# The last 64 down rows of a 2752-column FFN in a two-block transformer kernel: one 128-row pass over low and high parts in place of 64-row products

## The chip, the cores and the metric

The kernel runs on one core of one Trainium2 chip. The metric is the device time of one execution in microseconds (us). TensorE does the products, VectorE (DVE in the rows) and ScalarE (ACT) everything elementwise, and the Sync queue (SP) issues nearly all loads.

## The reference, cut to what matters

Two transformer blocks run one after the other on `x` of 1 x 256 x 1024 in float32. The first block has two layers, each of an FFN, a mixer and another FFN, so four FFNs of width `D_FF = 2752`:

```
def swiglu(x, w_gate, w_up, w_down):
    return (jax.nn.silu(x @ w_gate) * (x @ w_up)) @ w_down
x = x + 0.5 * swiglu(rms_norm(x, g[0]), ffn_w_gate[layer, 0], ffn_w_up[layer, 0], ffn_w_down[layer, 0])
```

`w_gate` and `w_up` are 1024 x 2752, `w_down` is 2752 x 1024. The second block has two more FFNs, of width 2816. 2752 is 21 times 128 and 64 more; 2816 is 22 times 128.

## The kernel before, in words

Each weight is read once, in units of at most 128 x 1024 floats (512 KB). `plan` lists the units in the order of their use. For each unit u, SP loads it into one of six staging buffers, as soon as unit u-6 has been split (`unit`, L2673 to 2688). ScalarE copies it into a high part `whi` in the rounded format fp32r (`split`, L1239; one of four buffers, so it waits for `used` of unit u-4). VectorE writes the rest into a low part `wlo` (L1733). Activations are held as high and low parts too. `three` (L600 to 602) then makes a product of three matmuls: high by high, high by low and low by high; low by low is left out.

An FFN runs in this order. `norm_T` transposes `xs` (L612) for k = 0 to 7, two transposes of 128 columns each. Ahead of k = 0 TensorE waits for the residual of token tile 1 and output half 0, ahead of k = 4 for that of tile 1 and half 1, which is the last of the four. ScalarE makes the high part `hTh` of each k (L1252), VectorE the low part `hTl` (through the helper at L1742), and the products of the next stage wait for these. Gate and up products follow by pairs of 128 columns. For each pair the hidden values are multiplied, and their high part `fh` (ScalarE, L1306 or L1310) and low part `fl` (VectorE, L1832 or L1840) are stored, transposed, in row tiles f = 0 to 21.

`down` walks the 22 row tiles of `w_down`. Four PSUM banks hold the output (two tiles t of 128 tokens by two halves n of 512 columns). For every row tile there are four groups of three matmuls, in the order n, then t. In the last row tile each group ends its bank, and VectorE adds the bank to `xs` (`residual`, L1742 for the four FFNs in question, L1783 for the mixers and for the first FFN of the second block): four additions, one after the other in VectorE's queue, followed there by the eight `hTl` of the next `norm_T`.

With F = 2752, `row_starts` gives the last unit the rows F-128 to F-1, of which the first 64 repeat rows already used. All operands of the last row tile are therefore cut to partitions 64 to 127 (`low`), in which the up products have also left the last 64 hidden values. The last pair of the up stage is special too (`if f.odd`): it has 128 + 64 columns, and its second half is worked on in partitions 64 to 127 alone.

Of the kernel before, what the change touches and what calls it, by code (L numbers as in the profile page):

```python
# [203 lines left out]
def build(nc, A, out):  # L204
    ctx = ExitStack()
    with ctx:
# [25 lines left out]
        def bk(*user):  # L232
            return PS[:, B.of[user], :]
# [49 lines left out]
        plan = []  # L283
# [34 lines left out]
                plan.append(([(0, cols(wg, k0, k0 + 4, c + 128, F), (4, 128), 0),  # L318
                              (0, cols(wu, k0, k0 + 4, c + 128, F), (4, 128), 64)], 512))

        def row_starts(F):
            r = [i * 128 for i in range(F // 128)]
            if F % 128:
                r.append(F - 128)
            return r

        def plan_down(w, F):
            plan_rows(w, row_starts(F))

        ffns = [(A["ffn_w_gate"][l, s], A["ffn_w_up"][l, s], A["ffn_w_down"][l, s], F1)  # L330
                for l in range(2) for s in range(2)]
# [54 lines left out]
        class Ffn:  # L386
            def __init__(self, g, i, gl, coef, c):
                self.g, self.gl, self.coef = g, gl, coef
                self.nf = len(row_starts(ffns[i][3]))
                self.odd = ffns[i][3] % 256 != 0  # L390
                self.pairs = self.nf // 2
                self.fh = sb(f"fh{i}", [128, 22, S], F32R, c)
                self.fl = sb(f"fl{i}", [128, 22, S], F32R, c)
                self.sg = [sb(f"sg{i}_{j}", [128, 2, 2 * S], c=c) for j in range(2)]

                self.rows = [(self.fh[:, f, :], self.fl[:, f, :],
                              low if self.odd and f == self.nf - 1 else everyrow, ("fl", g, f // 2))
                             for f in range(self.nf)]

        class Attend:  # L400

# [12 lines left out]
        class Even:  # L414
            def __init__(self, c):
                def al(shape, n=itertools.count()):
                    return sb(f"ev_{next(n)}", shape, c=c)

                self.g, self.gl = 1, 1
                self.mh = sb("ev_mh", [128, 8, S], F32R, c)  # L420
                self.ml = sb("ev_ml", [128, 8, S], F32R, c)
                self.u = sb("ev_u", [128, 4, PAD + S], c=c)
                self.acc = sb("ev_acc", [128, 4, S], c=c)
                self.taps = sb("ev_taps", [128, 4, PE_TAPS, 128], c=c)
                self.sq = sb("ev_sqc", [128, 4, S], c=c)
                self.rs = sb("ev_rs", [128, S], c=c)
                self.th = [sb(f"ev_th{i}", [128, 2 * S], c=c) for i in range(2)]
                self.qkv = sb("ev_qkv", [128, 2, 768], c=c)

                self.qT = sb("ev_qT", [128, 4, S], c=c)  # L430
                self.kT = sb("ev_kT", [128, 1, S], c=c)
                self.o = sb("ev_o", [128, 2, 512], c=c)
                self.cwr = sb("ev_cwr", [34, 512], c=c)
                self.hq = sb("ev_hq", [128, 2, 640], c=c)
                self.hr = sb("ev_hr", [128, 2, 8], c=c)
                self.hk = sb("ev_hk", [128, 2, 2], c=c)
                self.cw = sb("ev_cw", [128, 4, 34], c=c)
                self.vr = sb("ev_vr", [128, 4], c=c)
                self.qg = sb("ev_qg", [128, 2], c=c)
                self.sk = sb("ev_sk", [128, 8], c=c)  # L440
                self.skp = sb("ev_skp", [128, 8], c=c)
                qkv, qT, kT, hr = self.qkv, self.qT, self.kT, self.hr
                self.at = Attend("swa", 8, al, lambda h: qT[64 * (h % 2):64 * (h % 2) + 64, h // 2, :],
                                 lambda h: kT[64 * (h % 2):64 * (h % 2) + 64, 0, :],
                                 lambda kt, h: qkv[:, kt, 640 + (h % 2) * 64:704 + (h % 2) * 64],
                                 both_tiles("swa"), lambda t, h: hr[:, t, h:h + 1], self.o, sink=self.skp, apart=True, crossed=True)
                self.rows = [(self.mh[:, 4 + k, :], self.ml[:, 4 + k, :], everyrow, ("swa oT", k // 2))
                             for k in range(4)]
                self.rows += [(self.mh[:, k, :], self.ml[:, k, :], everyrow, ("ev ml",)) for k in range(4)]

        class Odd:
            def __init__(self, c):
                def al(shape, n=itertools.count()):
                    return sb(f"od_{next(n)}", shape, c=c)

                self.g, self.gl = 4, 4
                self.mh = sb("od_mh", [128, 8, S], F32R, c)
                self.ml = sb("od_ml", [128, 8, S], F32R, c)
                self.u = sb("od_u", [128, 4, 16 + S], c=c)
                self.w1 = [sb(f"od_w{i}", [128, 3, 16 + S], c=c) for i in range(2)]  # L460
                self.pl = sb("od_pl", [128, 4, S], c=c)
                self.pw = sb("od_pw", [128, 4, 128], c=c)
                self.qkv = sb("od_qkv", [128, 2, 1536], c=c)
                self.qT = sb("od_qT", [128, 4, S], c=c)
                self.kT = sb("od_kT", [128, 4, S], c=c)
                self.o = sb("od_o", [128, 2, 512], c=c)
                self.hq = sb("od_hq", [128, 2, 1024], c=c)
                self.hr = [sb(f"od_hr{i}", [128, 2, 8], c=c) for i in range(2)]
                self.psc = sb("od_psc", [128, 4], c=c)
                self.qg = sb("od_qg", [128, 2], c=c)  # L470
                qkv, qT, kT, hr = self.qkv, self.qT, self.kT, self.hr[0]
                self.at = Attend("dil", 8, al, lambda h: qT[64 * (h % 2):64 * (h % 2) + 64, h // 2, :],
                                 lambda h: kT[64 * (h % 2):64 * (h % 2) + 64, h // 2, :],
                                 lambda kt, h: qkv[:, kt, 1024 + h * 64:1088 + h * 64], both_tiles("dil"),
                                 lambda t, h: hr[:, t, h:h + 1], self.o, mult=both_tiles("mult"), apart=True,
                                 late=True)
                self.rows = [(self.mh[:, 4 + k, :], self.ml[:, 4 + k, :], everyrow, ("od ml",)) for k in range(4)]
                self.rows += [(self.mh[:, k, :], self.ml[:, k, :], everyrow, ("dil oT", k // 2)) for k in range(4)]

        class Mixer2:  # L480
            def __init__(self, l, g, c):
# [55 lines left out]

                self.place = [2, 6, 4, 0]
                self.rows = [(self.bh[:, self.place[k // 2] + k % 2, :], self.bl[:, self.place[k // 2] + k % 2, :],
                              everyrow, (P, "low", k // 2)) for k in range(8)]  # L540

            def N(self, a, b, t=None):
                return self.nat[:, :, W0 + a:W0 + b] if t is None else self.nat[:, t, W0 + a:W0 + b]
# [21 lines left out]
        def tensor_program(e):  # L565
# [131 lines left out]
            def down(g, rows, ahead=0):  # L697

                ps = {}
                for t in range(2):  # L700
                    for n in range(2):
                        ps[t, n] = room(("dn", g, t, n))
                for k, (h, lo, sl, step) in enumerate(rows[0:len(rows) - ahead]):
                    u, wh, wl = unit()
                    e.wait_ge(*K.at(*step))
                    last = k + 1 == len(rows)
                    for n in range(2):
                        cols_n = slice(n * 512, n * 512 + 512)
                        for t in range(2):
                            ts = slice(t * 128, t * 128 + 128)  # L710
                            m = three(ps[t, n], h[sl, ts], lo[sl, ts], wh[sl, cols_n], wl[sl, cols_n], k == 0, last)
                            steps = [("dn", g, t, n)] if last else []
                            if t and n:
                                steps.append(("used", u))
                            if steps:
                                m.then_inc(*K.inc("prod", *steps))
                            if last:
                                done("dn", g, t, n)
                        yield

            def ffn(f):
# [39 lines left out]
                for t in range(2):  # L761
                    ts = slice(t * 128, t * 128 + 128)
                    for n in range(2):
                        cols_n = slice(n * 512, n * 512 + 512)
                        for k in range(f.nf - 4, f.nf):
                            h, lo, sl, step = f.rows[k]
                            if k not in us:
                                us[k] = unit()
                                e.wait_ge(*K.at(*step))
                            u, wh, wl = us[k]  # L770
                            w = three(bk("dn", g, t, n), h[sl, ts], lo[sl, ts], wh[sl, cols_n], wl[sl, cols_n], False,
                                      k == f.nf - 1)
                        w.then_inc(*K.inc("prod", ("dn", g, t, n)))
                        done("dn", g, t, n)
# [947 lines left out]
        def vector_program(e):  # L1722
# [77 lines left out]
            def ffn(f):  # L1800
# [23 lines left out]
                def hidden(p):  # L1824
                    s = f.sg[p % 2]
                    e.wait_ge(*K.at("silu", g, p))
                    if f.odd and p == f.pairs - 1:
                        for j, sl in ((0, everyrow), (1, low)):
                            e.tensor_tensor(s[sl, j, 0:256], s[sl, j, 0:256], s[sl, j, 256:512], ALU.mult).then_inc(
                                *K.inc("mult", ("mult", g, p, j)))  # L1830
                            e.wait_ge(*K.at("fh", g, p, j))
                            e.tensor_tensor(f.fl[sl, 2 * p + j, :], s[sl, j, 0:256],  # L1832
                                            f.fh[sl, 2 * p + j, :].bitcast(F32),
                                            ALU.subtract).then_inc(*K.inc("fl", *([("fl", g, p)] if j else [])))
                        return
                    e.wait_ge(*K.at("scaled", g, p, "up"))
# [788 lines left out]
        def sync_program(e):  # L2625
# [51 lines left out]
            def unit(u):  # L2677
# [3 lines left out]
                for i, (off, src, shape, *at) in enumerate(parts):  # L2681
# [2 lines left out]
                        dst = dst.rearrange("p (a b) -> p a b", a=shape[0])  # L2684
                    for c in at:
                        dst = dst[:, :, c:c + src.shape[2]]
                    e.dma_start(dst, src).then_inc(
                        *K.dma(f"st{u % NS}", *([("st", u)] if i + 1 == len(parts) else [])))

# [58 lines left out]
```

## Time and profile before

| what | value |
|---|---|
| three executions, median (lowest to highest) | 1795.98 us (1795.02 to 1800.14) |
| profiled execution, its span; it has no other time | 1791.2 us |
| median less span | 4.8 us |
| TensorE busy | 1775.6 us, 99% |
| VectorE busy | 1272.9 us, 71% |
| ScalarE busy | 948.0 us, 53% |
| DMA queue of the loads | 56.5% of 16 engines |
| granted TensorE clock, mean | 1.000 |

A busy share covers each engine alone. The weight loads of TensorE (PEld) overlap its matmuls (PE), and each matmul's record is longer than the distance to the next one's start, as they are pipelined; so the distance of two starts is the cost of one in a stream.

### The profile page before, as it was taken

What the parts mean: (1) busy time and instruction counts of PE and PEld (TensorE: products, weight loads), DVE (VectorE), ACT (ScalarE), POOL (GpSimd) and SP (SyncE); (2) the same over time, 40 slices, a digit from 0 to 9 for tenths busy, and PEclk for the clock granted to TensorE, in tenths of its full rate; (3) what the DMA queues carried; (4) which work ended last, traced back from release to release, by engine and by line L of the source; (5) the groups of instructions that cost most, each with busy time, mean ns of one, the idle gap of its engine ahead of it and who ended that gap; (6) DMA issues with size and microseconds to landing.
All of it is one profiled execution on the core that took longest, in us unless ns stands there. A gap on an engine that the chain in (4) does not pass through costs nothing.

```text
span 1791.2 us, 24936 instructions
## 1 busy us (share of the span) xinstructions
PE 1775.6 (99%) x9718; PEld 1510.8 (84%) x9718; DVE 1272.9 (71%) x1933; ACT 948.0 (53%) x1346; POOL 30.2 (2%) x39
## 2 busy tenths in 40 slices
PE   9999999999999999999999999999999999999998
PEld 8888878888888888888888788888888878888887
DVE  7774795876577657677656977777756778677774
ACT  6554655555455545555545545455544644555553
POOL 0000000000000001000000000000000000000000
PEclk9999999999999999999999999999999999999999
DMA  8666523666566655366655544556666454456663
GB/s 274 190 181 201 173 71 116 190 177 202 174 195 186 196 166 187 108 200 186 194 177 179 180 119 131 180 181 189 189 192 172 141 156 129 152 188 190 189 195 109
DMA packets 227614, 309.25 MB, mean 173 GB/s; under 512 B 22494, under 2 KB 176254, under 8 KB 227498
## 3 DMA queue, kind: packets, MB, share of 16 engines
q1 hardware_dynamic: 227334, 307.35, 56.5%
q8 instruction: 78, 1.28, 0.3%
q10 hardware_dynamic: 164, 0.30, 0.1%
q14 instruction: 38, 0.31, 0.1%
HBM read 306.57 MB, written 1.05 MB: 172 GB/s over the span
## 4 chain that ended last, share of the span: by engine, by line
PE 91%; DVE 6%; ACT 2%; issue 1%; POOL 0%; POOLq 0%; ACTq 0%
PE ps L649 26%; PE ps L600 15%; PE ps L602 15%; PE ps L601 15%; PE ps L651 13%; DVE wlo L1733 2%; PE ps L1141 1%; PE ps L612 1%; PE ps L816 1%; DVE ev_acc L1742 1%; PE ps L842 1%; ACT whi L1239 1%; PE ps L829 1%; PE ps L784 0%; DVE m_scr L1742 0%
## 5 line engine op out<-in xcount | busy, mean ns | idle before, releaser
L1733 DVE TENSOR_TENSOR wlo<-staging,whi 128x1024 fp32r<-128x1024 f32 (+1 forms) x580 | 692.6, 1211 | 335.7 <-ACT whi L1239 335.3
L1239 ACT ACTIVATE whi<-staging 128x1024 fp32r<-128x1024 f32 (+1 forms) x580 | 606.3, 1050 | 475.5 <-PE ps L602 292.6
L649 PE MATMUL ps<-hT,whi 128*128 128x512 f32 x1984 | 624.1, 396 | 0.1
L651 PEld LDWEIGHTS ps<-hT,wlo 128*128 128x128 f32 x1984 | 372.7, 188 | 88.1
L651 PE MATMUL ps<-hT,wlo 128*128 128x256 f32 x1984 | 389.8, 278 | 0.0
L649 PEld LDWEIGHTS ps<-hT,whi 128*128 128x128 f32 x1984 | 302.1, 189 | 0.5 <-DVE wlo L1733 0.3
L600 PE MATMUL ps<-whi,fh 128*128 128x512 f32 (+1 forms) x520 | 202.8, 390 | 0.0
L601 PE MATMUL ps<-wlo,fh 128*128 128x512 f32 (+1 forms) x520 | 202.3, 389 | 0.0
L602 PE MATMUL ps<-whi,fl 128*128 128x512 f32 (+1 forms) x520 | 202.2, 389 | 0.0
L600 PE MATMUL ps<-whi,hT 128*128 128x512 f32 (+3 forms) x464 | 184.8, 398 | 0.8 <-DVE wlo L1733 0.6
L602 PE MATMUL ps<-whi,hT 128*128 128x512 f32 (+3 forms) x464 | 177.4, 382 | 0.0
L601 PE MATMUL ps<-wlo,hT 128*128 128x512 f32 (+3 forms) x464 | 177.0, 381 | 0.0
L600 PEld LDWEIGHTS ps<-whi,fh 128*128 128x128 f32 (+1 forms) x520 | 97.6, 188 | 21.4 <-DVE wlo L1733 1.4
L602 PEld LDWEIGHTS ps<-whi,fl 128*128 128x128 f32 (+1 forms) x520 | 97.5, 188 | 20.5
L601 PEld LDWEIGHTS ps<-wlo,fh 128*128 128x128 f32 (+1 forms) x520 | 97.6, 188 | 19.9
L600 PEld LDWEIGHTS ps<-whi,hT 128*128 128x128 f32 x464 | 87.2, 188 | 21.4 <-issue 3.8
L602 PEld LDWEIGHTS ps<-whi,hT 128*128 128x128 f32 x464 | 87.2, 188 | 16.3
L1310 ACT ACTIVATE fh<-sg 128x512 fp32r<-128x512 f32 x62 | 39.2, 632 | 114.0 <-DVE sg L1837 114.0
L601 PEld LDWEIGHTS ps<-wlo,hT 128*128 128x128 f32 x464 | 87.4, 188 | 14.3 <-issue 0.5
L1822 DVE TENSOR_TENSOR sg<-sg,R 128x512 f32<-128x512 f32 x124 | 85.9, 692 | 4.3
L1819 DVE TENSOR_TENSOR sg<-ps,sg 128x512 f32<-128x512 f32 x124 | 84.8, 684 | 0.2
L600 PE MATMUL ps<-hT,whi 128*128 128x256 f32 x288 | 82.8, 287 | 0.0
(344 smaller groups left out, 1887.7 us busy)
## 6 DMA issues: line engine op xcount, KB each, us to landing
staging<-in_w_in SPq DMA_DIRECT2D x92, 512.0 KB, 3.7
staging<-in_ffn_w_down SPq DMA_DIRECT2D x88, 512.0 KB, 4.2
staging<-in_ffn_w_gate SPq DMA_DIRECT2D x84, 512.0 KB, 4.5
staging<-in_ffn_w_up SPq DMA_DIRECT2D x84, 512.0 KB, 4.6
staging<-in_w_ffn_gate SPq DMA_DIRECT2D x44, 512.0 KB, 4.5
staging<-in_w_ffn_up SPq DMA_DIRECT2D x44, 512.0 KB, 4.5
staging<-in_w_ffn_down SPq DMA_DIRECT2D x44, 512.0 KB, 4.2
staging<-in_od_w_in SPq DMA_DIRECT2D x16, 512.0 KB, 3.7
```

Of the source, the lines that this page charges most:

```text
L600: e.matmul(o, lh, rh, start=start, stop=False)
L601: e.matmul(o, lh, rl, start=False, stop=False)
L602: return e.matmul(o, ll, rh, start=False, stop=stop)
L612: w = e.transpose(ps[:, t * 128:t * 128 + 128], xs[:, t, k * 128:k * 128 + 128], ident)
L649: e.matmul(o, wh[:, kk, j * 128:j * 128 + 128], hT[:, k, :], start=k == 0, stop=False)
L651: m = e.matmul(o[:, 0:256], wl[:, kk, j * 128:j * 128 + 128], hTh[:, k, :], start=False, stop=k == KD - 1)
L816: w = e.matmul(ops[t][:, (h0 + j) * 64:(h0 + j) * 64 + 64], a.pt[i % 2][:, o:o + 128], a.vN(kt, h0 + j), start=kt == 0, stop=kt == t)
L1239: e.activation(high(u)[:, 0:n], stage[u % NS][:, 0:n], ACT.Copy).then_inc(*K.inc("hi", ("hi", u)))
L1310: e.activation(f.fh[:, 2 * p:2 * p + 2, :], s[:, :, 0:256], ACT.Copy).then_inc(*K.inc("fh", ("fh", g, p, 0)))
L1733: e.tensor_tensor(low_of(u)[:, 0:n], stage[u % NS][:, 0:n], high(u)[:, 0:n].bitcast(F32), ALU.subtract).then_inc(*K.inc("lo", ("lo", u)))
L1819: e.tensor_tensor(ss, PS[:, b:b + 2, 0:256], ss, ALU.add).then_inc(*K.inc("ps_r", *[("ev", u) for u in users]))
L1822: e.tensor_tensor(ss, ss, R22, ALU.mult).then_inc(*K.inc("ps_r", ("scaled", g, p, part)))
```

## The change

The last unit of a 2752-column FFN holds the last 64 rows of `w_down` twice, in partitions 0 to 63 and in 64 to 127, by two DMAs of 256 KB. VectorE writes the low part of the last 64 hidden values not into `fl` but into partitions 0 to 63 of the last tile of `fh`, whose partitions 64 to 127 hold the high part. One product of this tile with `whi` then gives high by high and low by high, and one with `wlo` gives high by low and low by low: two matmuls of 128 rows for each of the four groups, in place of three of 64 rows. The `slice` member of each row entry is dropped. The number of units and their sizes stay.

```
+            plan_rows(w, [i * 128 for i in range(F // 128)])
             if F % 128:
+                assert F % 128 == 64
+                plan.append(([(0, w[F - 64:F, :], (1, 1024))] * 2, 1024))
...
+                self.rows = [(self.fh[:, f, :], None if self.odd and f == self.nf - 1 else self.fl[:, f, :],
+                              ("fl", g, f // 2)) for f in range(self.nf)]
...
-                for k, (h, lo, sl, step) in enumerate(rows[0:len(rows) - ahead]):
+                for k, (h, lo, step) in enumerate(rows[0:len(rows) - ahead]):
...
-                            m = three(ps[t, n], h[sl, ts], lo[sl, ts], wh[sl, cols_n], wl[sl, cols_n], k == 0, last)
+                            if lo is None:
+                                e.matmul(ps[t, n], h[:, ts], wh[:, cols_n], start=False, stop=False)
+                                m = e.matmul(ps[t, n], h[:, ts], wl[:, cols_n], start=False, stop=last)
+                            else:
+                                m = three(ps[t, n], h[:, ts], lo[:, ts], wh[:, cols_n], wl[:, cols_n], k == 0, last)
...
-                            e.tensor_tensor(f.fl[sl, 2 * p + j, :], s[sl, j, 0:256],
-                                            f.fh[sl, 2 * p + j, :].bitcast(F32),
+                            part = f.fh[top, 2 * p + 1, :] if j else f.fl[:, 2 * p, :]
+                            e.tensor_tensor(part, s[sl, j, 0:256], f.fh[sl, 2 * p + j, :].bitcast(F32),
...
+                    if src.shape[0] == 64:
+                        dst = dst[64 * i:64 * i + 64, :]
                     e.dma_start(dst, src).then_inc(
```

## Rows read from the trace of the kernel before

**Rows 1.** The page's busy times, their share of the span and the instructions.

```profile
PE 1775.6 (99%) x9718; PEld 1510.8 (84%) x9718; DVE 1272.9 (71%) x1933; ACT 948.0 (53%) x1346; POOL 30.2 (2%) x39
```

**Rows 2.** The page's chain that ended last, by engine and line.

```profile
PE 91%; DVE 6%; ACT 2%; issue 1%; POOL 0%; POOLq 0%; ACTq 0%
PE ps L649 26%; PE ps L600 15%; PE ps L602 15%; PE ps L601 15%; PE ps L651 13%; DVE wlo L1733 2%; PE ps L1141 1%; PE ps L612 1%; PE ps L816 1%; DVE ev_acc L1742 1%; PE ps L842 1%; ACT whi L1239 1%; PE ps L829 1%; PE ps L784 0%; DVE m_scr L1742 0%
```

**Rows 3.** Timeline, end of the first FFN (start us, us, engine, line), TensorE.

```profile
185.01 0.39 PE L600 MATMUL ps<-whi,fh 128*128 128x512 f32 x1
...
187.51 0.39 PE L602 MATMUL ps<-whi,fl 128*128 128x512 f32 x1
187.83 0.50 PE L600 MATMUL ps<-whi,fh 64*128 64x512 f32 x1
188.16 0.39 PE L601 MATMUL ps<-wlo,fh 64*128 64x512 f32 x1
188.40 0.39 PE L602 MATMUL ps<-whi,fl 64*128 64x512 f32 x1
...
190.45 0.39 PE L602 MATMUL ps<-whi,fl 64*128 64x512 f32 x1
190.77 2.01 PE L612 MATMUL ps<-cst,xs 128*128 128x128 f32 x16
```

**Rows 4.** The same, weight loads; in brackets idle time and releaser.

```profile
187.82 0.18 PEld L600 LDWEIGHTS ps<-whi,fh 64*128 64x128 f32 x1 [0.35 <-DVE wlo L1733]
...
192.70 0.19 PEld L600 LDWEIGHTS ps<-hT,whi 128*128 128x128 f32 x1 [0.16 <-DVE hT L1742]
```

**Rows 5.** The same, VectorE and ScalarE.

```profile
188.82 2.74 DVE L1742 SCALAR_TENSOR_TENSOR xs<-ps,xs 128x512 f32<-128x512 f32 x4 [1.23 <-PE ps L602]
191.75 2.44 DVE L1742 SCALAR_TENSOR_TENSOR hT<-ps,gcol,hT 128x256 fp32r<-128x256 f32 x6 [0.18 <-ACT hT L1252]
...
191.24 3.03 ACT L1252 ACTIVATE hT<-ps,gcol 128x256 fp32r<-128x256 f32 x8 [2.19 <-PE ps L612]
```

**Rows 6.** Timelines, ends of the second and the third FFN: last row's start, weight load after the transposes.

```profile
479.25 0.50 PE L600 MATMUL ps<-whi,fh 64*128 64x512 f32 x1
...
484.12 0.30 PEld L649 LDWEIGHTS ps<-hT,whi 128*128 128x128 f32 x2 [0.16 <-DVE hT L1742]
...
662.01 0.50 PE L600 MATMUL ps<-whi,fh 64*128 64x512 f32 x1
...
666.69 0.19 PEld L600 LDWEIGHTS ps<-whi,hT 128*128 128x128 f32 x1
```

**Rows 7.** Timelines, last down row of first second-block mixer: VectorE, weight loads.

```profile
1173.76 2.74 DVE L1783 TENSOR_TENSOR xs<-ps,xs 128x512 f32<-128x512 f32 x4 [1.02 <-PE ps L602]
1176.54 1.27 DVE L1742 SCALAR_TENSOR_TENSOR hT<-ps,gcol,hT 128x256 fp32r<-128x256 f32 x3
...
1176.62 0.86 PEld L612 LDWEIGHTS ps<-cst,xs 128*128 128x128 f32 x8 [0.21 <-DVE xs L1783]
1177.48 0.30 PEld L649 LDWEIGHTS ps<-hT,whi 128*128 128x128 f32 x2
```

**Rows 8.** Timelines, end of the second block's first FFN.

```profile
1358.67 2.73 DVE L1783 TENSOR_TENSOR xs<-ps,xs 128x512 f32<-128x512 f32 x4 [1.02 <-PE ps L602]
...
1362.34 0.19 PEld L600 LDWEIGHTS ps<-whi,hT 128*128 128x128 f32 x1
```

**Rows 9.** Issue of the first FFN's last down unit, and landing of all units.

```profile
165.86 0.33 SPq L2687 DMA_DIRECT2D staging<-in_ffn_w_down  x1
...
DMA to landing us min/median/max: 2.3/4.3/10.6
```

**Rows 10.** Timeline, the splits of that unit, ScalarE and VectorE.

```profile
179.84 1.06 ACT L1239 ACTIVATE whi<-staging 128x1024 fp32r<-128x1024 f32 x1 [1.66 <-PE ps L602]
...
180.93 1.23 DVE L1733 TENSOR_TENSOR wlo<-staging,whi 128x1024 fp32r<-128x1024 f32 x1 [1.50 <-ACT whi L1239]
```

**Rows 11.** Line 1296 of ScalarE: reads partitions 0 to 63, writes 64 to 127.

```profile
L1296 ACT ACTIVATE sg<-sg x4: 415/416/416, 134.9 to 880.2; 64x256 f32<-64x256 f32 x4
```

More of the change, by code:

```diff
@@ L319, in plan_up, with plan_down @@
                               (0, cols(wu, k0, k0 + 4, c + 128, F), (4, 128), 64)], 512))
-        def row_starts(F):
-            r = [i * 128 for i in range(F // 128)]
+        def plan_down(w, F):
+            plan_rows(w, [i * 128 for i in range(F // 128)])
             if F % 128:
[L324 to L328, printed above, removed]
+                assert F % 128 == 64
+                plan.append(([(0, w[F - 64:F, :], (1, 1024))] * 2, 1024))
         ffns = [(A["ffn_w_gate"][l, s], A["ffn_w_up"][l, s], A["ffn_w_down"][l, s], F1)
@@ L388, in __init__ @@
                 self.g, self.gl, self.coef = g, gl, coef
-                self.nf = len(row_starts(ffns[i][3]))
+                self.nf = -(-ffns[i][3] // 128)
                 self.odd = ffns[i][3] % 256 != 0
@@ L394, in __init__ @@
                 self.sg = [sb(f"sg{i}_{j}", [128, 2, 2 * S], c=c) for j in range(2)]
-                self.rows = [(self.fh[:, f, :], self.fl[:, f, :],
-                              low if self.odd and f == self.nf - 1 else everyrow, ("fl", g, f // 2))
-                             for f in range(self.nf)]
+                self.rows = [(self.fh[:, f, :], None if self.odd and f == self.nf - 1 else self.fl[:, f, :],
+                              ("fl", g, f // 2)) for f in range(self.nf)]
         class Attend:
@@ L446, in __init__ @@
                                  both_tiles("swa"), lambda t, h: hr[:, t, h:h + 1], self.o, sink=self.skp, apart=True, crossed=True)
-                self.rows = [(self.mh[:, 4 + k, :], self.ml[:, 4 + k, :], everyrow, ("swa oT", k // 2))
+                self.rows = [(self.mh[:, 4 + k, :], self.ml[:, 4 + k, :], ("swa oT", k // 2))
                              for k in range(4)]
-                self.rows += [(self.mh[:, k, :], self.ml[:, k, :], everyrow, ("ev ml",)) for k in range(4)]
+                self.rows += [(self.mh[:, k, :], self.ml[:, k, :], ("ev ml",)) for k in range(4)]
         class Odd:
@@ L476, in __init__ @@
                                  late=True)
-                self.rows = [(self.mh[:, 4 + k, :], self.ml[:, 4 + k, :], everyrow, ("od ml",)) for k in range(4)]
-                self.rows += [(self.mh[:, k, :], self.ml[:, k, :], everyrow, ("dil oT", k // 2)) for k in range(4)]
+                self.rows = [(self.mh[:, 4 + k, :], self.ml[:, 4 + k, :], ("od ml",)) for k in range(4)]
+                self.rows += [(self.mh[:, k, :], self.ml[:, k, :], ("dil oT", k // 2)) for k in range(4)]
         class Mixer2:
@@ L539, in __init__ @@
                 self.rows = [(self.bh[:, self.place[k // 2] + k % 2, :], self.bl[:, self.place[k // 2] + k % 2, :],
-                              everyrow, (P, "low", k // 2)) for k in range(8)]
+                              (P, "low", k // 2)) for k in range(8)]
             def N(self, a, b, t=None):
@@ L765, in ffn @@
                         for k in range(f.nf - 4, f.nf):
-                            h, lo, sl, step = f.rows[k]
+                            h, lo, step = f.rows[k]
                             if k not in us:
@@ L770, in ffn @@
                             u, wh, wl = us[k]
-                            w = three(bk("dn", g, t, n), h[sl, ts], lo[sl, ts], wh[sl, cols_n], wl[sl, cols_n], False,
+                            w = three(bk("dn", g, t, n), h[:, ts], lo[:, ts], wh[:, cols_n], wl[:, cols_n], False,
                                       k == f.nf - 1)
```

## The prediction

> **What bounds the kernel now.** I read the page's busy times first. TensorE is busy for 99% of the span [rows 1]. By itself that shows only that its queue never stands idle for long, since a matmul's record is longer than the distance to the next start. The chain of waits decides: 91% of it is TensorE, almost all in the product lines, with 6% VectorE and 2% ScalarE [rows 2]. So a matmul taken out of a stream is worth its distance to the next start, unless something else then ends last. The third view is therefore the timeline around the only place where products go away, the last down row of a 2752-column FFN.
>
> There, at the end of the first FFN, two things are to be seen. First, the 128-row matmuls start 0.227 us apart (11 steps from 185.01 to 187.51) and the 64-row ones, once in stream, 0.228 us apart (9 steps from 188.40 to 190.45) [rows 3]. Half the rows cost as much as all. Second, the 64-row stretch has edges: the first one starts 0.32 us after the last 128-row matmul, the second 0.33 us after the first, and the first transpose 0.32 us after the last product [rows 3]. That is three times about 0.1 us over the stream. The row of the weight load names VectorE's `wlo` for the first edge [rows 4], but the `wlo` of this very unit ended at 180.93 + 1.23 = 182.16 [rows 10], 5.7 us before. I take these edges as the price of going from 128 to 64 rows and back.
>
> **The change, part by part.** I measure from T, the start of the last row's first product in a plain stream: 187.51 + 0.227 = 187.74 in the first FFN. In the run before that product starts at 187.83.
>
> *Products.* Twelve of 64 rows become eight of 128. On TensorE alone the last row takes 190.77 - 187.74 = 3.03 us before [rows 3] and 8 x 0.227 = 1.82 us after, 1.21 us less. With four such FFNs that is 4.8 us.
>
> *What is late next.* The four residual additions of VectorE. They take 2.74 us for four, 0.685 us each, without a gap [rows 5]. Before, the groups of three products end every 0.68 us, so additions and products keep step. After, a group of two ends every 0.45 us, and the additions, one queue, fall behind. The first addition starts 0.42 us after the start of its group's last product (188.40 to 188.82 [rows 3, 5]), so after at T + 0.23 + 0.42 = T + 0.65. The second ends at T + 2.02, the fourth at T + 0.65 + 2.74 = T + 3.39. TensorE is done with the row at T + 1.82 and meets two waits in `norm_T`:
> - k = 0 waits for the second addition, T + 2.02. Before, it never waited there.
> - k = 4 waits for the fourth. The transposes of k = 0 to 3 are done about 0.9 us after T + 2.1, thus before T + 3.4.
>
> The price of this second wait can be read where the last row is a 128-row one already, in the mixers and in the wider FFNs. There the fourth addition ends at 1173.76 + 2.74 = 1176.50, the weight load of k = 4 starts at 1176.62 after 0.21 us of idleness put down to `xs`, and the next stage's first weight load at 1177.48 [rows 7]: 0.98 us after the fourth addition. That stage takes a pair of banks first, so it needs `hTl` of k = 0 and 1, as the stages after our first and second FFN do. Where the next stage takes one bank, as after our third and fourth, it is 1362.34 - (1358.67 + 2.73) = 0.94 us [rows 8].
>
> *Sum for one FFN.* First: after, the next stage's weight load comes at T + 3.39 + 0.98 = 187.74 + 4.37 = 192.11, before at 192.70 [rows 4], so 0.59 us less. The second FFN has the same distances (479.25 to 484.12 [rows 6], 4.87 us as from 187.83 to 192.70): 0.59. Third: T is 662.01 - 0.09 = 661.92, so 661.92 + 3.39 + 0.94 = 666.25 against 666.69 [rows 6]: 0.44. The fourth looks like the third: 0.44. Sum: 0.59 x 2 + 0.44 x 2 = 2.06 us. More than half of the 4.8 us of products turns into TensorE waiting for the additions.
>
> *Does the shift reach the end?* Every queue keeps its order and TensorE, VectorE and ScalarE all arrive earlier. VectorE's first `hTl` starts at about T + 3.42 = 191.16 instead of 191.75 [rows 5], 0.59 earlier. ScalarE's `hTh` starts 0.48 us after the first transpose (190.77 to 191.24 [rows 3, 5]), after at about T + 2.6 in place of T + 3.5. So the shift is kept also where the chain of the mixers runs over these two.
>
> *Loads.* One DMA of 512 KB becomes two of 256 KB. No row shows a load to half the partitions. From below it costs nothing. From above I take each of the two at the longest landing of any load, 10.6 us, one after the other: 21.2 us; the median is 4.3 [rows 9]. The unit is issued at 165.86 and its ScalarE copy starts at 179.84, after waiting for TensorE and not for the load [rows 9, 10]: 14.0 us. Then 5.6 us more lie between `wlo`'s end at 182.16 and T. I take zero, since twice the median is 8.6 us. The second issue costs SP 0.33 us [rows 9]. What is queued behind it is the next unit's load, with the same 14 us to spare.
>
> The Trainium skill, "DMA: Bandwidth & Descriptors", rules for kernel authors, speaks against this edit: two transfers to disjoint partition halves serialize on the same engines, and one of 128 partitions is to be used. By it the pair takes as long as its 512 KB do at present or somewhat longer, and the sum stays; it bears on the third rival alone. No row here shows such a pair.
>
> *VectorE's subtraction across halves.* It reads partitions 64 to 127 and writes 0 to 63. VectorE shows no such form, and the nearest row is ScalarE's crossing one, 0.416 us for 64 x 256 [rows 11]. I take no difference. A doubling would add about 0.4 us to VectorE once per FFN, and half of it would take 0.2 us away. The instruction stands ahead of VectorE's down rows, each of which leaves it 1.50 us idle [rows 10], so neither reaches the end.
>
> *The edges.* With 128 rows throughout, all three go. The two at the start of the row are worth between zero and 0.19 us of the fourth addition, 0.09 in T (187.74 for 187.83) and 0.10 in the first group (0.33 for 0.23 from its first to its second product), and the sum has both in full. The Trainium skill, "TensorEngine Tiling (Array Packing)", key properties, says that a change of tiling mode drains TensorE. By it the edges must vanish and the sum stands at 2.06 us; if they were something else, the second rival's 1.3 us would hold. Its rule agrees with the three edges in rows 3.
>
> Own time: the span goes from 1791.2 to 1789.1 us. The median lies 4.8 us above the span before, and I leave that unchanged: 1795.98 - 2.06 = 1793.9 us.
>
> **The rivals.**
> 1. *The whole 4.8 us arrives*, 1791.2 us: the additions don't bind, for instance because the transposes wait less than I read. Against it: k = 4 needs the fourth addition, and at the 128-row ends this wait is already there with 0.21 us [rows 7], although groups of three there end every 0.68 us (3 x 0.227). 7%.
> 2. *The edges stay.* Then T moves back by 0.09 and the first group by 0.10 more, and each FFN saves 0.19 us less: 0.40 x 2 + 0.25 x 2 = 1.3 us, 1794.7 us. For it: the row names `wlo` [rows 4]. Against: that was long done. 12%.
> 3. *Slower, by late loads.* Place: the wait of ScalarE's copy for the last down unit. It decides from the point where the pair lands more than 14.0 + 5.6 = 19.6 us after issue. At 21.2 us TensorE waits 1.6 us in each of the four FFNs, 6.4 us, against 2.06 gained: 1800.3 us. For it: only the unknown of half-partition loads. Against: it needs five times the median. 3%.
> 4. *The shift is lost on the way*, 1796.0 us: the stage behind is held by something that does not move, such as a `wlo` bound to loads. Against: two units are split ahead of each stage, and the chain never shows a load. 10%.
>
> The forecast itself has 64%. The last 4% I leave to what none of these names, half on each side.
>
> **How the numbers follow.** The time is that of the forecast, 1793.9 us. The cases from 1 to 4 without the third span 1791.2 to 1796.0. The three executions before lie 1 us below to 4 us above their median, so the median of the new kernel may sit a microsecond or more off its sum, more easily upwards. I set 1791.0 to 1797.0. Of one measurement of this kernel, 0.3% (5.4 us) can be told from no change; faster means below 1790.6 and slower above 1801.4. No case lies beyond either bound. For faster I give 6% (rival 1 with a little luck), for slower 4% (rival 3 and noise), for the same 90%.
>
> **What would show it.** In the profile after, the last row of the four FFNs has eight 128-row matmuls 0.227 us apart with no edge on either side. VectorE's four additions stay at 2.74 us in one piece and begin 0.65 us after the row. The transposes of `norm_T` are split by two idle stretches of TensorE put down to `xs`, the first about 0.3 us and the second about 0.4 us. The next stage starts 3.39 + 0.98 or 0.94 us after T. The loads of the pair land well before 14 us. The prediction is wrong if the wait at k = 4 does not grow (more gain), if the edges stay (less), or if the span falls by under 1 or over 3.5 us.

## The result

The changed kernel takes 1791.49 us in the median of 8 executions (1790.43 to 1794.82), the kernel before 1796.8 us in the 8 beside it (1795.02 to 1800.14). The ratio is 0.9978, with a 95% interval of 0.9969 to 0.9987. It is faster by 2.3 to 5.6 us, and within 0.3% of the kernel before at its midpoint. The prediction was 1793.9 us in a range of 1791.0 to 1797.0.

The page after, by the side of [rows 1, 2]: the matmuls are 9702 in place of 9718, and the chain is still TensorE's.

```profile
PE 1775.2 (99%) x9702; PEld 1511.4 (84%) x9702; DVE 1271.8 (71%) x1933; ACT 948.2 (53%) x1346; POOL 30.2 (2%) x39
...
PE 90%; DVE 6%; ACT 2%; issue 1%; SPq 0%; DMA 0%; POOL 0%; POOLq 0%; ACTq 0%; DVEq 0%
```

The timeline at the end of the first FFN answers to [rows 3]. Columns: start us, us, engine, line. The last row's eight products are L708 and L709.

```profile
188.14 0.39 PE L598 MATMUL ps<-whi,fl 128*128 128x512 f32 x1
188.37 0.39 PE L708 MATMUL ps<-whi,fh 128*128 128x512 f32 x1
188.59 0.39 PE L709 MATMUL ps<-wlo,fh 128*128 128x512 f32 x1
...
189.95 0.39 PE L709 MATMUL ps<-wlo,fh 128*128 128x512 f32 x1
190.45 2.26 PE L608 MATMUL ps<-cst,xs 128*128 128x128 f32 x16
```

T is 188.14 + 0.227 = 188.37, and the first product starts there: no edge. The second follows 0.22 us later, the eighth 7 x 0.226 after the first. But the first transpose comes 0.50 us after the eighth product and not 0.23. The weight loads answer to [rows 4], with the idle time ahead of each in brackets.

```profile
190.42 0.85 PEld L608 LDWEIGHTS ps<-cst,xs 128*128 128x128 f32 x8 [0.51 <-issue]
191.62 0.85 PEld L608 LDWEIGHTS ps<-cst,xs 128*128 128x128 f32 x8 [0.34 <-DVE xs L1742]
192.44 0.19 PEld L596 LDWEIGHTS ps<-hT,whi 128*128 128x128 f32 x1
```

Both waits of `norm_T` are there: 0.51 us ahead of k = 0, which the row puts down to "issue", and 0.34 us ahead of k = 4, put down to `xs`. The next stage's weight load comes 192.44 - 188.37 = 4.07 us after T; it was 192.70 - 187.74 = 4.96. VectorE and ScalarE, by the side of [rows 5]:

```profile
189.02 2.48 DVE L1742 SCALAR_TENSOR_TENSOR xs<-ps,xs 128x512 f32<-128x512 f32 x4 [0.80 <-PE ps L709]
191.42 2.44 DVE L1742 SCALAR_TENSOR_TENSOR hT<-ps,gcol,hT 128x256 fp32r<-128x256 f32 x6
...
190.90 3.03 ACT L1252 ACTIVATE hT<-ps,gcol 128x256 fp32r<-128x256 f32 x8 [1.21 <-PE ps L608]
```

The four additions start at T + 0.65 and take 2.48 us, not the 2.74 of before and of the prediction. The chain of waits (start us, us, what), shown for this place alone, goes over VectorE now, while in the kernel before it went over TensorE alone here:

```profile
188.75 0.24 PE ps L709
189.00 0.02 issue
189.02 2.48 DVE xs L1742 x4
191.50 2.35 DVE hT L1742 x6
```

At the third FFN (of [rows 6]) T is 665.05 - 0.65 = 664.40, and the next stage comes 4.07 us later again, in place of 4.77.

```profile
665.05 2.48 DVE L1742 SCALAR_TENSOR_TENSOR xs<-ps,xs 128x512 f32<-128x512 f32 x4 [0.80 <-PE ps L709]
...
668.47 0.19 PEld L596 LDWEIGHTS ps<-whi,hT 128*128 128x128 f32 x1
```

By these distances the change is worth 0.89 + 0.89 + 0.70 + 0.70 = 3.2 us. The span of this profiled execution is nevertheless 1792.3 us, longer than the 1791.2 before, because of 7 us at half the TensorE clock in the first mixer (last section). Its second profiled execution, e0 below, has none, and a span of 1788.0 us: 3.2 less.

### The profile page after: what moved, and what is told of

The parts are those of the page before. It is cut to its first block, busy times and chain, and to the rows that moved or that the text cites. A ratio compares the mean times of both kernels' runs of the same rounds, so it can differ in the third digit from the quotient of the medians.

```text
span 1792.3 us, 24908 instructions
## 1 busy us (share of the span) xinstructions
PE 1775.2 (99%) x9702; PEld 1511.4 (84%) x9702; DVE 1271.8 (71%) x1933; ACT 948.2 (53%) x1346; POOL 30.2 (2%) x39
## 4 chain that ended last, share of the span: by engine, by line
PE 90%; DVE 6%; ACT 2%; issue 1%; SPq 0%; DMA 0%; POOL 0%; POOLq 0%; ACTq 0%; DVEq 0%
PE ps L645 26%; PE ps L596 15%; PE ps L598 15%; PE ps L597 14%; PE ps L647 13%; DVE wlo L1733 2%; PE ps L1141 1%; PE ps L608 1%; PE ps L816 1%; DVE ev_acc L1742 1%; PE ps L842 1%; ACT whi L1239 1%; PE ps L829 1%; PE ps L784 0%; DVE m_scr L1742 0%
## 5 line engine op out<-in xcount | busy, mean ns | idle before, releaser
L596 PE MATMUL ps<-whi,fh 128*128 128x512 f32 x504 | 196.1, 389 | 0.0
L597 PE MATMUL ps<-wlo,fh 128*128 128x512 f32 x504 | 196.1, 389 | 0.0
L598 PE MATMUL ps<-whi,fl 128*128 128x512 f32 x504 | 196.1, 389 | 0.0
L598 PEld LDWEIGHTS ps<-whi,fl 128*128 128x128 f32 x504 | 94.6, 188 | 19.7
L596 PEld LDWEIGHTS ps<-whi,fh 128*128 128x128 f32 x504 | 94.6, 188 | 19.5
L597 PEld LDWEIGHTS ps<-wlo,fh 128*128 128x128 f32 x504 | 94.6, 188 | 19.3
```

The lines of the kernel that those rows point to most:

```text
L596: e.matmul(o, lh, rh, start=start, stop=False)
L597: e.matmul(o, lh, rl, start=False, stop=False)
L598: return e.matmul(o, ll, rh, start=False, stop=stop)
```

## The experiments

Two stretches carry the comparison, as neither holds a low clock in any trace: C from the first weight load after the second FFN to that after the third, and D from there to that after the fourth. Each holds one end of an FFN. All ratios are to the kernel before on the same chip.

| kernel | C, us | D, us | ratio, 95% interval |
|---|---|---|---|
| before | 182.57 | 271.12 | |
| changed (e0) | 181.89 | 270.41 | 0.9984, 0.9973 to 0.9995 |
| e1, loads alone | 182.57 | 271.09 | 1.0001, 0.9993 to 1.001 |
| e2, twelve of 128 rows | 182.36 | 270.85 | 0.9999, 0.999 to 1.0007 |
| e3, eight of 64 rows | 182.09 | 270.69 | 0.9998, 0.9988 to 1.0008 |
| e4, half additions | 181.27 | 269.76 | 0.9973, 0.996 to 0.9985 |
| e5, short row moved | 181.45 | 269.99 | 0.9983, 0.9973 to 0.9993 |
| e7, e5 and earlier parameters | 181.45 | 269.95 | 0.9967, 0.9955 to 0.9979 |
| e8, changed and earlier parameters | 181.87 | 270.38 | 0.9975, 0.9966 to 0.9984 |
| e9, changed | 181.89 | 270.39 | 0.9981, 0.997 to 0.9993 |
| e10, e7 again | 181.44 | 269.96 | 0.9964, 0.9952 to 0.9975 |

**e0, the changed kernel again.** No edit.

> The changed kernel once more, beside the others. Theory A (the last row costs fewer products, but VectorE's four additions are late next): against the kernel before 3.2 us less by the distances read in the trace, ratio 0.9982; in the trace the next stage's first weight load 4.07 us after the last row's start T. Theory B (every product taken out is worth its full distance and the additions cost nothing): ratio 0.9973 and 3.4 us after T.

0.68 us less in C, 0.71 in D, the next stage 4.07 or 4.08 us after T at all four ends, span 1788.0: theory A. Theory B's 3.4 us after T is nowhere.

**e1, the loads alone.**

```
-            plan_rows(w, row_starts(F))
+            plan_rows(w, row_starts(F)[0:F // 128])
+            if F % 128:
+                plan.append(([(0, w[F - 64:F, :], (1, 1024))] * 2, 1024))
```

> The loads alone: two DMAs of 64 rows for the last down unit, products as before (twelve of 64 rows). Theory A: the loads are hidden behind 14 us of lead, ratio 1.000 within 0.05%, distances at the end of the FFNs as before (4.96 and 4.77 us from T to the next stage's weight load). Rival (the pair lands late or disturbs the loads behind it): slower by 1 us and more, and ScalarE's copy of that unit waits for its load in the trace.

C and D are those of before within 0.03 us. In the table of DMA issues (KB each, us to landing) the half loads land like whole ones:

```profile
staging<-in_ffn_w_down SPq DMA_DIRECT2D x84, 512.0 KB, 4.2
...
staging<-in_ffn_w_down SPq DMA_DIRECT2D x8, 256.0 KB, 4.1
```

4.1 us each, of 14 us to spare. The third rival falls, and the loads are shown to be free here. The second FFN's row keeps its edges too.

**e2, the edges alone.**

```
                                 e.matmul(ps[t, n], h[:, ts], wh[:, cols_n], start=False, stop=False)
+                                e.matmul(ps[t, n], h[:, ts], wl[:, cols_n], start=False, stop=False)
                                 m = e.matmul(ps[t, n], h[:, ts], wl[:, cols_n], start=False, stop=last)
```

> The changed kernel with its third matmul put back: every group of the last row has three products of 128 rows, the one with the weights' low part done twice, so twelve and no 64-row form. It prices the edges alone. Theory A: no edge, groups every 0.68 us, next stage 4.59 and 4.55 us after T, as at the 128-row ends; against 4.96 and 4.77 before that is 0.37, 0.37, 0.22 and 0.22 us, 1.2 us in all, ratio 0.9993. Theory C (the edges belong to the last unit, not to the 64 rows): distances as before, ratio 1.000.

```profile
664.09 0.39 PE L708 MATMUL ps<-whi,fh 128*128 128x512 f32 x1
...
666.58 0.39 PE L710 MATMUL ps<-wlo,fh 128*128 128x512 f32 x1
666.81 2.10 PE L608 MATMUL ps<-cst,xs 128*128 128x128 f32 x16
...
664.97 2.05 DVE L1743 SCALAR_TENSOR_TENSOR xs<-ps,xs 128x512 f32<-128x512 f32 x3 [1.02 <-PE ps L710]
...
667.82 0.85 PEld L608 LDWEIGHTS ps<-cst,xs 128*128 128x128 f32 x8 [0.21 <-DVE xs L1743]
668.64 0.19 PEld L596 LDWEIGHTS ps<-whi,hT 128*128 128x128 f32 x1
```

T is 664.09 and the next stage 4.55 us later. The stretches lose 0.21 and 0.27 us, against 0.22 expected. At T no edge is left: the last product starts at 666.58 and the first transpose 0.23 us after it, so the third edge is gone too. So the edges come with the 64-row form, theory C falls, and they are about a third of the whole gain (by the expectation's terms 1.2 of 3.2 us). The median does not show it (0.9999, interval down to 0.999). Nine of its ten executions had a mean clock of 0.998 or less, of which more below; and in its trace a wait in the first mixer, found with e5, costs about 1.0 us.

**e3, fewer products, of 64 rows.**

```
+                            if sl is low:
+                                e.matmul(ps[t, n], h[sl, ts], wh[sl, cols_n], start=False, stop=False)
+                                m = e.matmul(ps[t, n], h[sl, ts], wl[sl, cols_n], start=False, stop=last)
+                            else:
                                 m = three(ps[t, n], h[sl, ts], lo[sl, ts], wh[sl, cols_n], wl[sl, cols_n], k == 0, last)
```

> Products alone, without the 128 rows: the last row has two products of 64 rows for each group, the product of the low part of the hidden values with the high part of the weights is left out. Theory A: the three edges of about 0.1 us stay, two of them ahead of the additions, so the next stage starts 0.19 us later than in the changed kernel: 4.26 us after T, 0.70, 0.70, 0.51 and 0.51 us less than before, 2.4 us in all, ratio 0.9987. If the edges were not due to the 64 rows but to the unit's place as the last, the changed kernel would have them too, which its trace does not show. Theory B: 3.6 us, ratio 0.9980.

```profile
664.39 0.39 PE L602 MATMUL ps<-whi,fl 128*128 128x512 f32 x1
664.71 0.50 PE L712 MATMUL ps<-whi,fh 64*128 64x512 f32 x1
665.04 0.39 PE L713 MATMUL ps<-wlo,fh 64*128 64x512 f32 x1
665.28 0.39 PE L712 MATMUL ps<-whi,fh 64*128 64x512 f32 x1
...
665.48 2.48 DVE L1746 SCALAR_TENSOR_TENSOR xs<-ps,xs 128x512 f32<-128x512 f32 x4 [1.00 <-PE ps L713]
...
668.90 0.19 PEld L600 LDWEIGHTS ps<-whi,hT 128*128 128x128 f32 x1
```

The two edges at the row's start are back (0.32 and 0.33 us), the additions start at T + 0.86 with T = 664.62, and the next stage is 4.28 us after T: 0.48 less than before in C and 0.43 in D, against 0.51 expected. The additions take 2.48 us here as well, so it is the two-product groups and not the 128 rows that let them run at their own pace. The ratio does not show the gain (0.9998 for an expected 0.9987, which lies below its interval), with ten of eleven executions at a mean clock of 0.998 or less.

**e4, the suspected limit cut.**

```
                 o, ps = xs[:, t, n * 512:n * 512 + 512], bk("dn", g, t, n)
+                if g in (0, 2, 3, 5):
+                    o, ps = o[:, 0:256], ps[:, 0:256]
```

> The changed kernel with the four residual additions of the 2752-column FFNs cut to the first 256 of their 512 columns. It takes away the suspected limit. Theory A: an addition takes about 0.42 us, less than the 0.45 us between groups; the fourth ends at about T + 2.4, and the next stage starts about 0.94 us later, 3.4 us after T in place of 4.07: 0.67 us less in each of the four, 2.7 us less than the changed kernel, ratio to before 0.9967. Theory B (additions never were in the way): still 4.07 us.

```profile
663.87 1.79 DVE L1742 SCALAR_TENSOR_TENSOR xs<-ps,xs 128x256 f32<-128x256 f32 x4 [0.80 <-PE ps L709]
...
664.87 1.84 PEld L608 LDWEIGHTS ps<-cst,xs 128*128 128x128 f32 x16
666.67 0.19 PEld L596 LDWEIGHTS ps<-whi,hT 128*128 128x128 f32 x1
```

This kernel leaves half of each sum out, so its output is wrong and only its times are of use. The additions end 0.65 + 1.79 = 2.44 us after T (663.22), the idle stretch ahead of k = 4 is gone, and the next stage comes 3.45 us after T. C and D are 0.62 and 0.65 us shorter than the changed kernel's (0.67 expected); this shows that the additions bound its end. At the first two FFNs the distance is 3.69 us and not 3.4. Their next stage needs two banks, and the first `hTl` now waits for ScalarE:

```profile
190.76 3.23 DVE L1742 SCALAR_TENSOR_TENSOR hT<-ps,gcol,hT 128x256 fp32r<-128x256 f32 x8 [0.30 <-ACT hT L1252]
...
191.70 0.19 PEld L596 LDWEIGHTS ps<-hT,whi 128*128 128x128 f32 x1 [0.20 <-DVE hT L1742]
```

The expectation had left that out. Once the additions are out of the way, the next limit at the first two FFNs is ScalarE's `hTh`: VectorE stands idle 0.30 us for it, and TensorE 0.20 us for `hTl`. At the third and fourth it is TensorE's own 16 transposes, which run in one piece up to the next stage (664.87 + 1.84 = 666.71). The ratio, 0.9973, is short of the 0.9967 expected, which lies within its interval; its trace has the longest but one of the waits that e5 is about.

**e5, the short row one place forward.**

```
-                plan.append(([(0, w[F - 64:F, :], (1, 1024))] * 2, 1024))
+                plan.insert(-1, ([(0, w[F - 64:F, :], (1, 1024))] * 2, 1024))
...
+                if self.odd:
+                    self.rows[-2:] = self.rows[:-3:-1]
```

> The changed kernel with its short last row moved one place forward: the 64 last rows come as the last but one unit, a full row of twelve products ends the banks. Theory A: the groups of the last row come every 0.68 us again, slower than an addition of 0.60, so the additions keep up: next stage 2.72 + 1.87 = 4.59 us after the last row's start, that is 1.82 + 4.59 = 6.41 us after the start of the last two rows, against 2.72 + 4.07 = 6.79 us in the changed kernel. 0.38 us less in each of four FFNs, 1.5 us: ratio to before 0.9974. Theory B: the same as the changed kernel, as the products are the same.

```profile
660.07 2.74 DVE L1744 SCALAR_TENSOR_TENSOR xs<-ps,xs 128x512 f32<-128x512 f32 x4
...
662.92 0.86 PEld L610 LDWEIGHTS ps<-cst,xs 128*128 128x128 f32 x8 [0.21 <-DVE xs L1744]
663.75 0.19 PEld L598 LDWEIGHTS ps<-whi,hT 128*128 128x128 f32 x1
```

The same products, in another order: 0.44 us less in C and 0.42 in D, as 6.79 - (1.82 + 4.55) = 0.42 would have it. The additions hide behind the products again, and theory B falls a second time. But the ratio is no better than the changed kernel's. One reason may be the clock: eight of its eleven executions had a mean of 0.998 or less, against four of eleven in e0. Another is in a third stretch, B, from the weight load after the first FFN to T of the second (in e5 T is set 2.72 us after the start of the last two rows, so that both orders count alike): 478.61 - 191.46 = 287.2 us here and 478.16 - 191.72 = 286.4 in e0. The list of waits from 193 to 212 us (engine, line, who was waited for: us, times, longest) names a load, first in e5, then in the changed kernel, then in e4:

```profile
PE ps L894 <- DMA ev_sk<-in_ev_sinks: 1.0, 1, 1.0
```

```profile
PE ps L892 <- DMA ev_sk<-in_ev_sinks: 0.7, 1, 0.7
```

```profile
PE ps L892 <- DMA ev_sk<-in_ev_sinks: 2.2, 1, 2.2
```

Before it was 0.2 us, in e0 none, and in e2, which arrives later than e0, 1.3 us. TensorE waits there for nine small parameter loads of the first mixer, and how late they land differs from one execution to the next by more than a microsecond. B grows with this wait. Where a trace has a low clock in B, what it costs is taken off as in the last section: 286.5 us before, 286.4 in e0, 286.7 in the changed kernel's first trace (0.7 us of wait), 287.4 in e2 and 288.3 in e4.

**e7 and e8, the parameter loads earlier.** e7 is e5 with this edit, e8 the changed kernel with it.

```
-            before = {first[1] + 10: (even_load, evs), ...
+            before = {first[1] + 8: (even_load, evs), ...
```

> The kernel with the short row moved one place forward, and in addition the small parameter loads of the first mixer issued two units earlier. In the trace of the former TensorE waited 1.0 us for them at 204 us (0.2 us in the kernel before, 0.7 and 0.0 us in two traces of the changed one). Theory D (this wait, set by loads and not by the shifted queues, ate the gain of the first FFN): the wait is gone, and the stretch from the first FFN's end to the second's last row is 0.7 us shorter than with the swap alone (286.4 for 287.2 us). Rival: the wait only looks so, and the stretch stays 287.2 us. Ratio to before by theory D 0.9970.

> The changed kernel with the small parameter loads of the first mixer issued two units earlier, nothing else. Theory D: no wait of TensorE for them; the stretch from the first FFN's end to the second's last row is 286.4 us as in the trace of the changed kernel that did not wait, so at most 0.3 us less than the changed kernel in the mean, ratio to before 0.9981. Rival: moving nine small loads ahead of two weight loads makes those late, and the mixer longer than 286.4 us.

In both traces the first of these loads is issued at 190.6 and 190.7 us, where it was 198.0 in the changed kernel and 197.0 in e5, and no wait of TensorE for a load is left in the list. In e8, without a low clock, B is 286.4 us as expected, and the rival with late weight loads falls. In e7 it is 289.65 us with a low clock in it; less 3 x (0.27 + 0.50 + 0.36) = 3.4 us, from its windows of 3 us as in the last section, it is 286.3, against 287.2 in e5. e10, the same kernel again, gives 481.30 - 191.66 = 289.64, less 3.4 us again 286.2. So theory D holds, though in e7 and e10 by corrected numbers only.

**e9 and e10, the pair once more.** The changed kernel and e7, side by side.

> The changed kernel again, as the partner of the next on the same chip. 3.2 us less than before, ratio 0.9982.

> The kernel with the short row one place forward and the first mixer's parameter loads two units earlier, again, beside the changed kernel. By the distances of the traces it is 0.38 x 2 + 0.42 x 2 = 1.6 us faster than the changed kernel, 4.8 us faster than the kernel before: ratio to before 0.9973, and 0.9991 to the changed one. If the gain of the short row's new place is lost again elsewhere, both ratios to before agree.

0.9981 and 0.9964. C and D are 0.45 and 0.43 us shorter in e10. Together with e7 (0.9967) the version of e7 beats the kernel before by 0.2 to 0.5%. Against the changed kernel its advantage is clear in the traces; of the ratios, the intervals (0.997 to 0.9993 and 0.9952 to 0.9975) still overlap.

## Why the prediction was right, and by which step it was too small

The sign, the size class and the mechanism held: the products fell by 1.2 us per FFN, the additions of VectorE took their place as the limit, and TensorE now waits at k = 0 and k = 4.

- *Products and edges*: as said. Eight products 0.227 us apart, no edge. e2 and e3 price the two parts apart. The two idle stretches in `norm_T`, 0.51 and 0.34 us, had been put at 0.3 and 0.4.
- *Start of the additions*, T + 0.65: as said.
- *Duration of the additions*: the mis-sized term. I took 2.74 us from [rows 5] as VectorE's own pace, since the four stand in one piece. It was the pace of the products, 3 x 0.227 = 0.68 us a group. A record of 0.69 us hides that the next one may start earlier. The four take 2.48 us when nothing holds them, so (2.48 - 0.69) / 3 = 0.60 us each: 0.26 us less at each end. The trace of before had a step of the same size elsewhere (a TENSOR_TENSOR without PSUM), whose record is 0.69 us and behind which the next one starts after 0.61 us:

```profile
110.44 0.69 DVE L1822 TENSOR_TENSOR sg<-sg,R 128x512 f32<-128x512 f32 x1
111.05 1.22 DVE L1733 TENSOR_TENSOR wlo<-staging,whi 128x1024 fp32r<-128x1024 f32 x1
```

- *From the fourth addition to the next stage*: 0.94 us at all four ends. I had 0.98 for the first two, 0.04 too much. With both corrections 2.06 + 2 x 0.30 + 2 x 0.26 = 3.2 us, what the traces have.
- *Does the shift reach the end?* Not always in full. The fourth rival (something behind that does not move) is partly true: TensorE waited for the parameter loads of the first mixer 0.7 us in one trace of the changed kernel and not at all in e0; B, less 3.4 us of low clock, is 286.66 us in the first and 286.44 in the second, so 0.2 us was lost. In e5 it was 0.7 us. e7 and e8 took the wait away. I had argued from weight units alone and had not looked at the small loads in the same queue.
- *Loads*: free, as said (e1).
- *Subtraction across halves*: free, as said. It takes 0.420 us, where the same 64 x 256 within one half took 0.42 us before. The view of its line (ns min/median/max):

```profile
L1833 DVE TENSOR_TENSOR fh<-sg,fh x4: 420/420/421, 141.6 to 888.2; 64x256 fp32r<-64x256 f32 x4
```

- *Own time*: 4.8 us above the span was wrong. In every execution with both numbers the time is the span plus 2.1 to 2.2 us. The profiled execution before held full clock; about half of the timed ones in the later sets did not, and the rest of the 4.8 us is of that kind and size (the granted clock of the first three is not known).

That the number stayed inside its range is in part luck. The median, 1791.49 us, lies 2.4 us below the forecast, 0.5 us above the range's lower end and only 0.3 us from the first rival's 1791.2, so by itself it would have spoken for that rival. Of the 2.4 us, 1.1 are the mis-sized terms. The other 1.3 are not in the traces: the two medians of the result are 5.3 us apart where the distances give 3.2, and the prediction had no term for the clock, which the last section suggests as their source. One sign that the prediction named, a span that falls by under 1 us, even came to pass in the first trace (1791.2 to 1792.3 us), for the same want of a term for the clock; in e0, without a low clock, the span fell by 3.2.

The first rival (4.8 us) is refuted by the two waits in the trace and by e4, the second (edges stay) by the trace and e2, the third by e1.

## What to carry to other kernels

Removing products at the end of an accumulation shortens the interval between finished banks. Once it is under the time that the engine which empties them needs for one, the saving is capped, and a short step is better put where a full one follows it. Take an engine's pace from a place where it is surely not waiting: a row of several instructions in one piece may still be paced by whoever feeds them. And when a stage gets earlier, look for the loads issued on a condition of their own, small ones included, as they do not move with it.

## What the runs showed of the hardware

*A drop of the clock.* In the profiled execution of the changed kernel the granted clock is at 0.50 for some 7 us in the first mixer. Views: busy time of each engine in two stretches (us, then PE, PEld, DVE, ACT, POOL, clock, DMA share, GB/s), and two matmuls in it.

```profile
240.00:260.00 20.00, 17.94 (x98) 14.11 (x97) 19.40 (x69) 8.36 (x28) 0.00 (x0) 1.00 0.10 29
276.00:279.00 3.00, 3.00 (x12) 2.79 (x12) 1.12 (x5) 1.23 (x1) 0.70 (x1) 0.50 0.00 0
```

```profile
278.22 0.63 PE L597 MATMUL ps<-wlo,ev_mh 128*128 128x512 f32 x1
278.65 0.63 PE L598 MATMUL ps<-whi,ev_ml 128*128 128x512 f32 x1
```

Matmuls follow each other after 0.43 us in place of 0.227, which is 1.2 in place of 2.4 GHz. In the windows of 3 us from 273 to 285 the clock is 0.97, 0.50, 0.50 and 0.89, so 3 x (0.03 + 0.50 + 0.50 + 0.11) = 3.4 us are lost. Ahead of it TensorE had been less busy than elsewhere, 17.94 of 20 us from 240 to 260; but the kernel before has 17.93 there and e0 17.70, and both keep full clock. What decides it is open. Eight of the twelve traces have such a stretch between 273 and 285 us, which costs 1.7 to 3.4 us each; the trace of before, e0, e5 and e8 have none. As e1, with the products of before, is one of the eight, and e0 and e8, with those of the changed kernel, are not, it does not come with the change alone.

*A second place.* The profiled execution of e9 waited longest for the parameter loads, 2.8 us, and has a low clock right behind that wait as well (the wait, and the windows; columns as above):

```profile
PE ps L892 <- DMA ev_sk<-in_ev_sinks: 2.8, 1, 2.8
```

```profile
201.00:204.00 3.00, 2.94 (x25) 2.75 (x24) 1.25 (x2) 1.18 (x2) 0.00 (x0) 1.00 0.36 44
204.00:207.00 3.00, 0.24 (x3) 0.27 (x3) 0.66 (x1) 0.64 (x1) 0.00 (x0) 0.84 1.03 349
207.00:210.00 3.00, 3.00 (x10) 2.39 (x10) 2.48 (x6) 0.12 (x1) 0.00 (x0) 0.50 0.50 162
210.00:213.00 3.00, 3.00 (x9) 2.34 (x8) 2.71 (x7) 0.82 (x3) 0.00 (x0) 0.52 0.61 177
```

That is 3 x (0.16 + 0.50 + 0.48) = 3.4 us more. e2 and e4, with waits of 1.3 and 2.2 us, keep full clock there, so one trace shows it and no more. If it is more than chance, the earlier parameter loads save this too, which would fit that e8 and e7 gained more in their ratios (0.9975, 0.9967) than their distances give (0.9982, 0.9973); this was not tested by itself.

*What that does to a median.* The kernel before, in 72 executions of the three sets of experiments: 37 with a mean clock of 0.999 or 1.000, median 1794.33 us; 35 lower, median 1797.60. The changed kernel, 30: 17 and 13, medians 1791.11 and 1794.82. Class by class the gain is 3.2 and 2.8 us, near the 3.2 of the traces, while the two medians of the result are 5.3 us apart. One execution of e9 took 6947 us and is in none of these numbers. In e3 and e2 the lower clock holds in 19 of 21 executions, which can hide gains of 1 to 2 us in their medians. Compared in the same set at the same rounded mean clock, e3 is 1.6 (0.997) and 1.0 us (0.998) under the kernel before in the mean, e2 1.0 and 0.5 us, from three to seven executions on each side: less than the 2.4 and 1.2 expected, but of their sign. Whether the kernels cause that or chance does, these runs do not settle.

*Half loads.* A DMA of 256 KB into 64 partitions took 3.7 to 4.1 us to land, one of 512 KB into 128 partitions 4.1 to 4.2.
